# FFN up projection with the weights stationary and 256 tokens moving

## The chip, the core and the metric

The kernel runs on one core of a Trainium2 chip. Five engines of a core take part. TensorE does matmuls, VectorE, ScalarE and GpSimd work on elements, and SyncE issues most transfers. The metric is the device time of one run in microseconds (us). All arithmetic is on f32 data. A product of two f32 matrices is made of three TensorE passes in the type fp32r: each operand is split into a high part (a cast to fp32r) and a low part (the rest), and the passes are high x high, high x low and low x high.

## The reference, cut to what matters

Two layers, 256 tokens, model width 2048, feed-forward width 8192. What the change touches is the last line but one:

```python
def hybrid_layer(x, ...):
    ...
    mixed = jnp.concatenate([rms_norm(attn, g_attn_out), rms_norm(pool, g_pool_out)], axis=-1) @ w_out
    x = x + rms_norm(mixed, g_mix_post)
    f = jnp.square(jax.nn.relu(rms_norm(x, g_ffn_pre) @ w_up)) @ w_down
    return x + rms_norm(f, g_ffn_post)
```

`rms_norm(x, g)` is x times g over the root of the mean square of a token's row. The kernel applies g before the projection and the row's scale (`rstd`, one number a token) to its result.

## The kernel before, in words

**Tiles.** The 256 tokens are two halves (t = 0, 1) of 128. A weight matrix is taken in units of 512 output columns; a unit has 2048 rows of weights, in 8 slots of two blocks of 128 rows. Half 0 of a unit is slots 0 to 3, half 1 is slots 4 to 7. The feed-forward part of a layer is four groups (`group`, line 641). A group is four up units (512 features each) and then four down units that use these 2048 features.

**Weights.** SyncE loads 512 KB pieces into four buffers `raw` (line 303), each when VectorE has finished with the buffer. ScalarE casts a piece into `w_hi` (`split_hi`, line 687) once it has landed and TensorE has released the slot (`w_used`). VectorE subtracts it to make `w_lo` (`split_lo`, line 959), and TensorE waits for that (`lo_made`).

**A unit on TensorE** (`unit`, line 385, and `pair`, line 360). It goes first through all 8 slots for t = 0, then through all 8 for t = 1. A pair is one slot for one t and holds six passes. The stationary operand (128 x 128) is a block of tokens, and the moving operand is 512 columns of weights. The result is tokens on partitions and 512 features in one bank, `acc_bank[t]`. In the code, (n, p) counts the pairs: n = 0, 1 are the halves for t = 0, n = 2, 3 those for t = 1, and p is the slot of a half. The first pass of a bank waits for `acc_free[t]`, by which whoever reads the last result says that it is taken. A slot is released after its pair for t = 1, so all slots are needed in the first half of a unit and released in the second.

**After an up unit.** ScalarE reads the bank with relu and the row scale (line 902) and squares it (line 906). TensorE turns the 128 x 512 result in four transposes (`turn_f`, line 631) so that the features lie on partitions, as the down projection needs them for its stationary operand. ScalarE copies the turned bank as `f_hi` (line 911), VectorE makes `f_lo` (line 1221). The turn of t = 1 stands at (1, 2) of the following unit, the turn of t = 0 at (3, 2) of its own.

**After a down unit.** VectorE adds the bank into `acc` (`down_sum`, lines 1232 and 1234). The order that VectorE keeps in a down unit is written out:

```python
                    with dve.Fori(0, CHUNKS - 1 if last else CHUNKS) as c:
                        down_sum(g, c, 0, first)
                        split_lo(hu + 8 + c * 2 + 2, 0)
                        split_lo(hu + 8 + c * 2 + 3, 1)
                        down_sum(g, c, 1, first)
```

Each engine runs its instructions in the written order, and semaphores tie them together.

**The first up unit of a layer.** Its tokens for t = 1 are made ready while it runs (`h_first_unit`, line 410). The row scale of t = 1 comes late in it. ScalarE squares x (line 713) and does four casts, VectorE does four subtractions and then the mean (`mean_x`, line 1001; line 979), and GpSimd takes the root (line 1316). Before the change only ScalarE waits for this scale, in `activate` for t = 1.

## Time and profile before

| what | value |
|---|---|
| median of 3 runs | 2082.39 us (2081.54 to 2083.51) |
| span of the profiled execution | 2081.2 us |
| TensorE matmul busy | 2046.5 us, 98% |
| TensorE weight load busy | 1695.0 us, 81% |
| VectorE busy | 1088.2 us, 52% |
| ScalarE busy | 998.6 us, 48% |
| GpSimd busy | 212.1 us, 10% |

The page of the profile gives the span and no other time of that execution. Engines are named PE (TensorE matmul), PEld (TensorE weight load), DVE (VectorE), ACT (ScalarE), POOL (GpSimd) and SP (SyncE); L377 is line 377 of the kernel. Matmuls are pipelined, so the duration of one is longer than the distance to the next, and their ends are modelled. Starts are the better guide.

### The profile page before, as it was taken

The page shows a single profiled execution, that of the slowest core. Times are in us where ns is not written, and L with a number is a line of the kernel's source. Part 1 is how long each engine was busy: PE and PEld are TensorE (multiplying, and loading weights), DVE is VectorE, ACT ScalarE, POOL GpSimd, SP SyncE. Part 2 cuts the span into 40 slices and gives each one's busy share as a digit, 9 for nine tenths or more (in the row PEclk, how much of TensorE's full clock was granted, in tenths as well). Part 3 has the DMA queues.
Part 4 walks back from the last instruction along what each step waited for, and adds up shares of the span by engine and source line. Part 5 has one row for each costly group of instructions (what it writes and reads, how often), then busy time and mean ns, then how long its engine had stood idle before and what let it go on. Part 6 is the DMA issues. An engine that isn't in the chain of part 4 may idle for free.

```text
span 2081.2 us, 28816 instructions
## 1 busy us (share of the span) xinstructions
PE 2046.5 (98%) x9298; PEld 1695.0 (81%) x9298; DVE 1088.2 (52%) x1105; ACT 998.6 (48%) x1247; POOL 212.1 (10%) x248
## 2 busy tenths in 40 slices
PE   7999999999999999999989999999999999999998
PEld 5888887888888888888878888878888888888886
DVE  6554657554554554554554446664454454454454
ACT  5444656543553453454454446565345444444542
POOL 3951014000000000000120010230000000000001
PEclk9999999999999999999999999999999999999999
DMA  6664454565565555655556544555565566466463
GB/s 214 222 207 137 140 184 160 177 205 186 181 196 188 187 189 188 213 191 182 165 195 208 191 142 130 166 185 183 185 202 191 173 202 200 162 195 230 161 196 128
DMA packets 196518, 381.65 MB, mean 183 GB/s; under 512 B 11904, under 2 KB 14048, under 8 KB 195808
## 3 DMA queue, kind: packets, MB, share of 16 engines
q1 hardware_dynamic: 195776, 379.12, 55.7%
q10 hardware_dynamic: 672, 1.61, 0.2%
q8 instruction: 42, 0.69, 0.1%
q14 instruction: 28, 0.23, 0.0%
HBM read 378.59 MB, written 2.10 MB: 183 GB/s over the span
## 4 chain that ended last, share of the span: by engine, by line
PE 48%; issue 41%; POOL 8%; DMA 1%; DVE 0%; POOLq 0%; ACT 0%; SPq 0%; ACTq 0%; DVEq 0%
PE acc_bank L377 16%; PE acc_bank L379 16%; PE acc_bank L378 16%; POOL acc L1324 2%; POOL h_lo L1297 1%; PE t_bank L637 1%; POOL f_lo L1297 1%; DMA post_row<-in_g_ffn_post 1%; DMA x<-in_x 1%; POOL rstd L1316 0%; PE t_bank L405 0%; POOL band L1453 0%; POOL band L1447 0%; POOL tmp L1417 0%; POOL tmp L1423 0%
## 5 line engine op out<-in xcount | busy, mean ns | idle before, releaser
L964 DVE TENSOR_TENSOR w_lo<-raw,w_hi 128x1024 fp32r<-128x1024 f32 x704 | 871.5, 1250 | 573.4 <-ACT w_hi L692 538.9
L692 ACT CAST w_hi<-raw 128x1024 fp32r<-128x1024 f32 x704 | 734.1, 1052 | 481.7 <-PE acc_bank L379 265.9
L377 PE MATMUL acc_bank<-w_hi,h_hi 128*128 128x512 f32 x1536 | 608.9, 396 | 3.9 <-POOL h_lo L1297 2.2
L379 PE MATMUL acc_bank<-w_hi,h_lo 128*128 128x512 f32 x1536 | 600.0, 391 | 0.0
L378 PE MATMUL acc_bank<-w_lo,h_hi 128*128 128x512 f32 x1536 | 599.3, 390 | 0.0
L377 PE MATMUL acc_bank<-w_hi,f_hi 128*128 128x512 f32 x1216 | 477.4, 393 | 0.0
L379 PE MATMUL acc_bank<-w_hi,f_lo 128*128 128x512 f32 x1216 | 473.5, 389 | 0.0
L378 PE MATMUL acc_bank<-w_lo,f_hi 128*128 128x512 f32 x1216 | 473.1, 389 | 0.0
L377 PEld LDWEIGHTS acc_bank<-w_hi,h_hi 128*128 128x128 f32 x1536 | 289.8, 189 | 65.4 <-DVE w_lo L964 4.0
L379 PEld LDWEIGHTS acc_bank<-w_hi,h_lo 128*128 128x128 f32 x1536 | 289.0, 188 | 61.3
L378 PEld LDWEIGHTS acc_bank<-w_lo,h_hi 128*128 128x128 f32 x1536 | 289.7, 189 | 57.9
L379 PEld LDWEIGHTS acc_bank<-w_hi,f_lo 128*128 128x128 f32 x1216 | 228.2, 188 | 47.9
L378 PEld LDWEIGHTS acc_bank<-w_lo,f_hi 128*128 128x128 f32 x1216 | 228.4, 188 | 46.6
L377 PEld LDWEIGHTS acc_bank<-w_hi,f_hi 128*128 128x128 f32 x1216 | 228.3, 188 | 46.3
L1324 POOL TENSOR_TENSOR acc<-acc,post_row 128x512 f32<-128x512 f32 x32 | 43.2, 1353 | 1369.0 <-ACT junk L872 1369.0
L911 ACT CAST f_hi<-t_bank 128x512 f32 x64 | 37.6, 587 | 216.7 <-PE t_bank L637 216.7
L1221 DVE TENSOR_TENSOR f_lo<-t_bank,f_hi 128x512 f32 (+1 forms) x64 | 44.3, 692 | 186.0 <-ACT f_hi L911 186.0
L902 ACT ACTIVATE act_f<-acc_bank,rstd 128x512 f32<-128x512 f32 x64 | 43.8, 685 | 99.0 <-PE acc_bank L379 99.0
L1234 DVE TENSOR_TENSOR acc<-acc_bank,acc 128x512 f32 (+1 forms) x48 | 33.0, 688 | 99.2 <-PE acc_bank L379 99.2
L872 ACT ACTIVATE junk<-acc 128x512 f32<-128x512 f32 (+1 forms) x32 | 20.2, 632 | 93.0 <-DVE acc L1234 58.2
L1297 POOL TENSOR_TENSOR h_lo<-xg,h_hi 128x512 fp32r<-128x512 f32 x32 | 55.3, 1749 | 38.6 <-ACT h_hi L697 38.6
L1297 POOL TENSOR_TENSOR f_lo<-xg,f_hi 128x512 fp32r<-128x512 f32 x16 | 20.5, 1293 | 339.8 <-ACT f_hi L697 339.8
(150 smaller groups left out, 822.2 us busy)
## 6 DMA issues: line engine op xcount, KB each, us to landing
raw<-in_w_up SPq DMA_DIRECT2D x256, 512.0 KB, 4.4
raw<-in_w_down SPq DMA_DIRECT2D x256, 512.0 KB, 5.4
raw<-in_w_in SPq DMA_DIRECT2D x128, 512.0 KB, 4.8
raw<-in_w_out SPq DMA_DIRECT2D x64, 512.0 KB, 5.3
w_pool_s<-in_w_pool SPq DMA_DIRECT2D x2, 1024.0 KB, 8.5
post_row<-in_g_mix_post SPq DMA_DIRECT2D x2, 1024.0 KB, 7.3
post_row<-in_g_ffn_post SPq DMA_DIRECT2D x2, 1024.0 KB, 7.9
out<-x SPq DMA_DIRECT2D x8, 256.0 KB, 2.7
```

What stands on the lines that cost most here:

```text
L377: pe.matmul(bank[:, :], xh, wh, start=begin and k == 0, stop=False)
L378: pe.matmul(bank[:, :], xh, wl, start=False, stop=False)
L379: mm = pe.matmul(bank[:, :], xl, wh, start=False, stop=end and k == 1)
L637: tr = pe.transpose(t_bank[t][:, h_cols(j)], act_f[:, t, h_cols(j)], ident[:, :])
L692: act.copy(w_hi[:, half * PAIRS + p, :], raw[:, p, :]).then_inc(hi_made, 1)
L902: act.activation(act_f[:, t, :], acc_bank[t][:, :], ACT.Relu, scale=rstd[:, COL_X2 + t:COL_X2 + t + 1]).then_inc(acc_free[t], 1)
L911: act.copy(f_out(f_hi, u, t), t_bank[t][:, :].rearrange("p (k n) -> p k n", k=4)).then_inc(fhi_made, 1)
L964: dve.tensor_tensor(w_lo[:, slot, :], raw[:, p, :], w_hi[:, slot, :].bitcast(F32), ALU.subtract).then_inc(lo_made, 1)
L1221: dve.tensor_tensor(f_out(f_lo, u, t), t_bank[t][:, :].rearrange("p (k n) -> p k n", k=4), f_out(f_hi, u, t).bitcast(F32), ALU.subtract).t ...
L1234: dve.tensor_tensor(dst, acc_bank[t][:, :], dst, ALU.add).then_inc(acc_free[t], 1)
L1297: pool.tensor_tensor(lo, xg[:, slot, :].rearrange("p (k n) -> p k n", k=k), hi.bitcast(F32), ALU.subtract).then_inc(st_lo, 1)
L1324: pool.tensor_tensor(part, part, post_row[:, c_cols(c)], ALU.mult).then_inc(post_ready, 1)
```

## The change

All up units but the first of a layer change their order. A block of 128 x 128 weights is now the stationary operand and all 256 tokens are the moving one. One unit is 8 slots; a slot is four blocks of 128 features (n), two blocks of rows (k) and three passes of 256 columns, 24 passes in all. The result has features on partitions: blocks n = 0, 1 lie in the first bank of a pair of banks, n = 2, 3 in the second. Units take `acc_bank` and `s_bank` by turns (`up_bank`), so these units need no transposes. A slot is released as soon as its 24 passes are issued.

With tokens along the free axis the row scale is no longer one number a partition. In the first unit TensorE spreads it over the partitions (`spread_rstd`, before pair (3, 1)), and VectorE copies it to `rstd_row`. VectorE then takes an up result with relu and the row scale in one operation (`take_up`). ScalarE squares and casts it, VectorE subtracts (`up_lo`). The loop over the units of a group is written out in the program instead of a loop of the engine, on TensorE, ScalarE and VectorE. The first down unit takes `acc_bank`, while the last up unit lies in `s_bank`; hence its `spare`. In the cut below, empty lines are left out.

```diff
@@ -82,7 +82,7 @@
 TB_F = 18
-TB_LAYER = TB_F + FF_GROUPS * CHUNKS
+TB_LAYER = TB_F + 1
 XG_Y = 8
@@ -185,6 +185,7 @@
     act_f = at("act_f", [P, T, CH], F32, r_qkv)
+    rstd_row = at("rstd_row", [P, SEQ], F32, r_qkv + 4 * (T + 1) * CH + 4 * T * CH)
     post_row = own("post_row", [P, D])
@@ -272,9 +275,16 @@
     ld = bass.ds
-    def f_out(dst, u, t):
-        return dst[:, ld(u * 4, 4), h_cols(t)]
+    def f_turned(dst, t):
+        return dst[:, 0:4, h_cols(t)]
+    def f_part(dst, u, b):
+        return dst[:, 4 * u + 2 * b:4 * u + 2 * b + 2, :]
+    def up_bank(u, b):
+        return (acc_bank, s_bank)[u % 2][b]
     def result_stands(eng, t, result, hu):
...
-            def unit(hu, result, hi, lo, before=None):
+            def unit(hu, result, hi, lo, before=None, spare=0):
...
-                    pe.wait_ge(acc_free[t], result + 1)
+                    pe.wait_ge(acc_free[t], result + 1 - spare)
@@ -628,41 +638,75 @@
                                     h_turns(l, 1, (2, 3))
-                def turn_f(g, u, t):
-                    pe.wait_ge(f_ready, l * 32 + g * 8 + u * 2 + t + 1)
-                    pe.wait_ge(flo_made, l * 32 + g * 8 + u * 2 + t + 1)
+                def turn_first(t):
+                    pe.wait_ge(f_ready, l * T + t + 1)
                     for j in range(4):
                         tr = pe.transpose(t_bank[t][:, h_cols(j)], act_f[:, t, h_cols(j)],
                                           ident[:, :])
                     tr.then_inc(tb_done[t], 1)
+                def spread_rstd():
+                    pe.wait_ge(rstd_ready, T + l * RS_LAYER + RS_X2 + T)
+                    for t in range(T):
+                        mm = pe.matmul(o_bank[:, h_cols(t)],
+                                       rstd[:, COL_X2 + t:COL_X2 + t + 1].to_broadcast([P, P]),
+                                       ident[:, :], start=True, stop=True)
+                    mm.then_inc(row_done, 1)
+                def up_unit(hu, u, result, before=None):
+                    for s in range(2 * PAIRS):
+                        half, p = s // PAIRS, s % PAIRS
+                        if before is not None:
+                            before(s)
+                        pe.wait_ge(lo_made, (hu + half) * PAIRS + p + 1 + RAW)
+                        for n in range(4):
+                            b = n // 2
+                            dst = up_bank(u, b)[:, (n % 2) * SEQ:(n % 2 + 1) * SEQ]
+                            if s == 0 and n % 2 == 0:
+                                pe.wait_ge(acc_free[b], result + (1 if u == 0 else 0))
+                            for k in range(2):
+                                kt = 2 * s + k
+                                col = k * CH + n * P
+                                wh = w_hi[:, s, col:col + P]
+                                wl = w_lo[:, s, col:col + P]
+                                begin = s == 0 and k == 0 and n % 2 == 0
+                                end = s == 2 * PAIRS - 1 and k == 1 and n % 2 == 1
+                                pe.matmul(dst, wh, h_hi[:, kt, :], start=begin, stop=False)
+                                pe.matmul(dst, wh, h_lo[:, kt, :], start=False, stop=False)
+                                mm = pe.matmul(dst, wl, h_hi[:, kt, :], start=False, stop=end)
+                            if s == 2 * PAIRS - 1 and n == 1:
+                                mm.then_inc(acc_done, 1)
+                        mm.then_inc(w_used, 1)
                 def group(g, first, last):
                     hu = hu0 + HU_F + g * HU_GROUP
                     r = a0 + ACC_F + g * (2 * CHUNKS)
-                    h_before = h_first_unit(l, 1) if first else None
-                    def up_first(n, p):
-                        if h_before is not None:
+                    if first:
+                        h_before = h_first_unit(l, 1)
+                        def up_first(n, p):
                             h_before(n, p)
-                        if (n, p) == (3, 2):
-                            turn_f(g, 0, 0)
-                    unit(hu, r, h_hi, h_lo, up_first)
-                    with pe.Fori(1, CHUNKS) as u:
-                        def up_next(n, p):
-                            if (n, p) == (1, 2):
-                                turn_f(g, u - 1, 1)
+                            if (n, p) == (3, 1):
+                                spread_rstd()
                             if (n, p) == (3, 2):
-                                turn_f(g, u, 0)
-                        unit(hu + u * 2, r + u, h_hi, h_lo, up_next)
+                                turn_first(0)
+                        unit(hu, r, h_hi, h_lo, up_first)
+                    for u in range(1 if first else 0, CHUNKS):
+                        def up_next(s):
+                            if first and u == 1 and s == 1:
+                                turn_first(1)
+                        up_unit(hu + u * 2, u, r + u, up_next)
                     def down_first(n, p):
-                        if (n, p) == (1, 2):
-                            turn_f(g, CHUNKS - 1, 1)
-                        if p == 0:
-                            pe.wait_ge(flo_made, T + l * 32 + g * 8 + (3, 7, 4, 8)[n])
+                        if n < 2:
+                            pe.wait_ge(flo_made, l * 32 + g * 8 + max(2, 4 * n + p + 1))
                     def down_last(n, p):
@@ -670,7 +714,8 @@
                                 h_turns(l + 1, 0, (0, 1) if n == 2 else (2, 3))
-                    unit(hu + 2 * CHUNKS, r + CHUNKS, f_hi, f_lo, down_first)
+                    unit(hu + 2 * CHUNKS, r + CHUNKS, f_hi, f_lo, down_first, 1)
                     with pe.Fori(1, CHUNKS - 1 if last else CHUNKS) as c:
@@ -894,37 +939,51 @@
                 mix_square(1, 3)
-                def activate(g, u, t):
+                def activate_first(t):
                     act.wait_ge(rstd_ready, T + l * RS_LAYER + RS_X2 + t + 1)
-                    result_stands(act, t, a0 + ACC_F + g * 8 + u,
-                                  hu0 + HU_F + g * HU_GROUP + u * 2 + 1)
+                    result_stands(act, t, a0 + ACC_F, hu0 + HU_F + 1)
                     act.activation(act_f[:, t, :], acc_bank[t][:, :], ACT.Relu,
                                    scale=rstd[:, COL_X2 + t:COL_X2 + t + 1]
                                    ).then_inc(acc_free[t], 1)
-                    act.wait_ge(acc_free[t], 1 + a0 + ACC_F + g * 8 + u + 1)
+                    act.wait_ge(acc_free[t], 1 + a0 + ACC_F + 1)
                     act.activation(act_f[:, t, :], act_f[:, t, :], ACT.Square
                                    ).then_inc(f_ready, 1)
-                def f_chunk_hi(g, u, t):
-                    act.wait_ge(tb_done[t], l * TB_LAYER + TB_F + g * 4 + u + 1)
-                    act.copy(f_out(f_hi, u, t), t_bank[t][:, :].rearrange("p (k n) -> p k n", k=4)
+                def turned_hi(t):
+                    act.wait_ge(tb_done[t], l * TB_LAYER + TB_F + 1)
+                    act.copy(f_turned(f_hi, t), t_bank[t][:, :].rearrange("p (k n) -> p k n", k=4)
                              ).then_inc(fhi_made, 1)
+                def up_first(hu):
+                    activate_first(0)
+                    split_hi(hu + 2, 0)
+                    turned_hi(0)
+                    split_hi(hu + 3, 1, (0, 1, 2))
+                    activate_first(1)
+                    split_hi(hu + 3, 1, (3,))
+                    turned_hi(1)
                 def up_unit(g, u, hu):
-                    activate(g, u, 0)
                     split_hi(hu + 2, 0)
-                    f_chunk_hi(g, u, 0)
-                    split_hi(hu + 3, 1, (0, 1, 2))
-                    activate(g, u, 1)
-                    split_hi(hu + 3, 1, (3,))
-                    f_chunk_hi(g, u, 1)
+                    split_hi(hu + 3, 1)
+                    i = l * 2 * (FF_GROUPS * CHUNKS - 1) + 2 * (g * CHUNKS + u - 1)
+                    for b in range(2):
+                        act.wait_ge(acc_free[b], 1 + a0 + ACC_F + g * 8 + u + 1)
+                        act.activation(act_f[:, b, :], act_f[:, b, :], ACT.Square
+                                       ).then_inc(squared, 1)
+                        act.wait_ge(squared, i + b + 1)
+                        act.copy(f_part(f_hi, u, b),
+                                 act_f[:, b, :].rearrange("p (k n) -> p k n", k=2)
+                                 ).then_inc(fhi_made, 1)
                 def group(g, first, last):
                     hu = hu0 + HU_F + g * HU_GROUP
                     if first:
                         h_first_unit(l, 1, hu)
-                    with act.Fori(0, CHUNKS) as u:
+                        up_first(hu)
+                    for u in range(1 if first else 0, CHUNKS):
                         up_unit(g, u, hu + u * 2)
@@ -1014,7 +1073,6 @@
             dve.sem_inc(lo_made, RAW)
-            dve.sem_inc(flo_made, T)
             dve.memset(ones[:, :], 1.0).then_inc(ones_made, 1)
@@ -1215,13 +1273,36 @@
                 split_lo(hu_f + 1, 1, (1,))
-                def f_chunk_lo(g, u, t):
-                    dve.wait_ge(fhi_made, l * 32 + g * 8 + u * 2 + t + 1)
-                    dve.tensor_tensor(f_out(f_lo, u, t),
+                def turned_lo(t):
+                    dve.wait_ge(fhi_made, l * 32 + t + 1)
+                    dve.tensor_tensor(f_turned(f_lo, t),
                                       t_bank[t][:, :].rearrange("p (k n) -> p k n", k=4),
-                                      f_out(f_hi, u, t).bitcast(F32), ALU.subtract
+                                      f_turned(f_hi, t).bitcast(F32), ALU.subtract
                                       ).then_inc(flo_made, 1)
+                def take_row():
+                    dve.wait_ge(row_done, l + 1)
+                    dve.tensor_copy(rstd_row[:, :], o_bank[:, 0:SEQ]).then_inc(row_ready, 1)
+                def take_up(g, u):
+                    for b in range(2):
+                        result_stands(dve, b, a0 + ACC_F + g * 8 + u,
+                                      hu0 + HU_F + g * HU_GROUP + u * 2 + 1)
+                        dve.scalar_tensor_tensor(
+                            act_f[:, b, :].rearrange("p (k n) -> p k n", k=2),
+                            up_bank(u, b)[:, :].rearrange("p (k n) -> p k n", k=2), 0.0,
+                            rstd_row[:, None, :].to_broadcast([P, 2, SEQ]), ALU.max, ALU.mult
+                            ).then_inc(acc_free[b], 1)
+                def up_lo(g, u):
+                    for b in range(2):
+                        dve.wait_ge(fhi_made, l * 32 + g * 8 + u * 2 + b + 1)
+                        dve.tensor_tensor(f_part(f_lo, u, b),
+                                          act_f[:, b, :].rearrange("p (k n) -> p k n", k=2),
+                                          f_part(f_hi, u, b).bitcast(F32), ALU.subtract
+                                          ).then_inc(flo_made, 1)
                 def down_sum(g, c, t, first):
@@ -1237,19 +1318,21 @@
                     hu = hu0 + HU_F + g * HU_GROUP
-                    def up_unit(u, at_start):
-                        split_lo(hu + u * 2 + 2, 0)
-                        if at_start:
-                            mean_x(l, 1, 1)
-                        f_chunk_lo(g, u, 0)
-                        split_lo(hu + u * 2 + 3, 1)
-                        f_chunk_lo(g, u, 1)
                     if first:
                         h_first_unit(l, 1, hu)
-                        up_unit(0, True)
-                    with dve.Fori(1 if first else 0, CHUNKS) as u:
-                        up_unit(u, False)
+                        split_lo(hu + 2, 0)
+                        mean_x(l, 1, 1)
+                        turned_lo(0)
+                        take_row()
+                        split_lo(hu + 3, 1)
+                        turned_lo(1)
+                        dve.wait_ge(row_ready, l + 1)
+                    for u in range(1 if first else 0, CHUNKS):
+                        split_lo(hu + u * 2 + 2, 0)
+                        split_lo(hu + u * 2 + 3, 1, (0, 1, 2))
+                        take_up(g, u)
+                        split_lo(hu + u * 2 + 3, 1, (3,))
+                        up_lo(g, u)
                     with dve.Fori(0, CHUNKS - 1 if last else CHUNKS) as c:
```

## Rows read from the trace of the kernel before

**Rows 1.** The page, part 1: busy time, share of the span, instructions.
```profile
PE 2046.5 (98%) x9298; PEld 1695.0 (81%) x9298; DVE 1088.2 (52%) x1105; ACT 998.6 (48%) x1247; POOL 212.1 (10%) x248
```
**Rows 2.** Groups: line, engine, names, count, busy us, mean ns, idle before.
```profile
L377 PE MATMUL acc_bank<-w_hi,h_hi 128*128 128x512 f32 x1536 | 608.9, 396 | 3.9 <-POOL h_lo L1297 2.2 <-issue 0.8 <-DVE w_lo L964 0.7
...
L637 PE MATMUL t_bank<-ident,act_f 128*128 128x128 f32 x256 | 38.3, 271 | 0.0
```
**Rows 3.** Timeline (start us, us, engine, line), TensorE in a down unit.
```profile
800.02 0.39 PE L378 MATMUL acc_bank<-w_lo,f_hi 128*128 128x512 f32 x1
...
802.74 0.39 PE L378 MATMUL acc_bank<-w_lo,f_hi 128*128 128x512 f32 x1
```
**Rows 4.** Windows: busy us (count) by engine, clock, DMA; up phase, group 1.
```profile
507.10:597.50 90.40, 90.40 (x413) 74.80 (x413) 43.73 (x40) 44.81 (x53) 0.00 (x0) 1.00 0.56 184
```
**Rows 5.** Timeline, TensorE around the first turn of an up unit.
```profile
347.83 0.40 PE L379 MATMUL acc_bank<-w_hi,h_lo 128*128 128x512 f32 x1
348.06 0.60 PE L637 MATMUL t_bank<-ident,act_f 128*128 128x128 f32 x4
...
348.74 0.39 PE L378 MATMUL acc_bank<-w_lo,h_hi 128*128 128x512 f32 x1
```
**Rows 6.** Timeline, weight loads of eight short plain f32 operations, three places.
```profile
231.41 1.02 PEld L528 LDWEIGHTS t_bank<-ident,probs 128*128 128x128 f32 x8
232.40 0.19 PEld L377 LDWEIGHTS acc_bank<-w_hi,f_hi 128*128 128x128 f32 x1
...
239.03 1.71 PEld L517 LDWEIGHTS s_bank<-qk_t 128*128 128x128 f32 x8
240.76 0.19 PEld L377 LDWEIGHTS acc_bank<-w_hi,f_hi 128*128 128x128 f32 x1
...
277.24 1.08 PEld L620 LDWEIGHTS ssa_bank<-ones,o_sqsum 128*128 128x128 f32 x8
278.24 0.19 PEld L377 LDWEIGHTS acc_bank<-w_hi,f_hi 128*128 128x128 f32 x1
```
**Rows 7.** Timeline at the start of an up group, first and last of six.
```profile
507.14 0.39 PE L377 MATMUL acc_bank<-w_hi,h_hi 128*128 128x512 f32 x1
...
508.94 1.05 ACT L692 CAST w_hi<-raw 128x1024 fp32r<-128x1024 f32 x1 [0.23 <-DMA raw<-in_w_up]
...
507.46 3.79 DVE L964 TENSOR_TENSOR w_lo<-raw,w_hi 128x1024 fp32r<-128x1024 f32 x3 [1.10 <-ACT w_hi L692]
511.17 0.68 DVE L1232 COPY acc<-acc_bank 128x512 f32 x1
...
1893.76 0.39 PE L377 MATMUL acc_bank<-w_hi,h_hi 128*128 128x512 f32 x1
...
1898.45 0.68 DVE L1234 TENSOR_TENSOR acc<-acc_bank,acc 128x512 f32 x1
```
**Rows 8.** Timeline of the first up unit; last row: the same in layer 1.
```profile
346.47 0.39 PE L379 MATMUL acc_bank<-w_hi,h_lo 128*128 128x512 f32 x1
...
352.66 0.15 DVE L979 TENSOR_SCALAR_CACHE_REDUCE ss_x<-ss_x 128x4 f32<-128x4 f32 x1
...
352.90 0.55 POOL L1316 TENSOR_TENSOR rstd<-mean_sq,minus_half 128x1 f32<-128x1 f32 x1 [7.86 <-DVE ss_x L979]
...
1383.66 0.55 POOL L1316 TENSOR_TENSOR rstd<-mean_sq,minus_half 128x1 f32<-128x1 f32 x1 [7.86 <-DVE ss_x L979]
```
**Rows 9.** Timeline and windows (clock third from the end) after two idle times.
```profile
32.12 0.50 PE L377 MATMUL acc_bank<-w_hi,h_hi 128*128 128x512 f32 x1 [2.16 <-POOL h_lo L1297]
...
332.43 1.97 PE L405 MATMUL t_bank<-ident,x 128*128 128x128 f32 x8 [2.40 <-DVE x L991]
...
332.00:335.50 3.50, 3.07 (x12) 2.78 (x13) 3.50 (x7) 1.47 (x5) 0.04 (x1) 0.53 0.41 139
...
32.40:35.50 3.10, 3.10 (x19) 2.60 (x19) 1.35 (x3) 0.41 (x1) 1.36 (x1) 1.00 0.02 5
```
**Rows 10.** The page, part 3: a queue of instructions, packets, MB, share.
```profile
q8 instruction: 42, 0.69, 0.1%
```

6 lines of the change are left out of this document (4 added, 2 removed).

## The prediction

> **What bounds the kernel now.** I read the busy shares first: TensorE works for 98% of the span [rows 1], so time can come or go only through what TensorE issues and what it waits for. The grouped lines come next. They say how many passes there are of each kind, and that hardly any idle time stands before them [rows 2]. They do not give the cost of a pass, since its recorded duration (396 ns) overlaps the next one. The pace is read from start times instead: twelve passes of 512 columns from 800.02 to 802.74, or 226.7 ns each [rows 3]. An up phase of four units lasts 90.40 us [rows 4]. Its 4 x 96 passes are 87.05 us of that, and its seven blocks of four turns are the other 3.35 us, 0.48 us a block. The timeline agrees: 347.83 to 348.74 is 0.91 us for two passes and a block, so 0.46 us for the block, and the passes behind it are a little slow [rows 5]. So the up phase is TensorE alone, with nothing in it that waits.
>
> **Passes.** 30 units (15 of each layer) go from 96 passes of 512 columns to 192 of 256. The columns stay the same, but there are twice as many weight loads and twice as many pass starts. Before: 2880 x 0.2267 = 652.9 us. After: 5760 times a pace that the trace does not show for these operands, so I bound it.
> The load alone is one bound. Eight loads with one moving column each take 277.24 to 278.24. The first one begins with the pass before it (0.227), so the other seven cost 0.110 us each [rows 6]. No pace below about 110 ns has a row with this kind of operand.
> The stream is the other bound. Plain f32 turns with 128 columns take (0.99 - 0.227)/7 = 0.109 each, and plain f32 passes with 256 columns take (1.73 - 0.227)/7 = 0.215 [rows 6]. That is a line of 0.83 ns a column and 2.5 ns a pass, with the load hidden behind the stream in both. If the passes of this kernel have the same 2.5 ns fixed, their columns cost (226.7 - 2.5)/512 = 0.438 ns, and 256 columns cost 114.6 ns. If instead the whole surcharge over the ideal stream (226.7 - 213.3 = 13.4 ns, with 2.4 GHz being the granted clock of 1.00 in the window [rows 4]) falls on each pass or on each load, 256 columns cost 106.7 + 13.4 = 120.0 ns.
> I take 114.6, because it is built on the only two sizes of one kind that the trace has: 660.1 us, **+7.2 us**. The ends are 110 ns (633.6 us, -19.3) and 120 ns (691.2 us, +38.3).
> The Trainium skill (TensorE: Matmul & The Clock Gate, Back-to-back issue gap) gives a warm gap of columns/2.4 + 2.5 ns. For 256 columns that is an estimate of 109.2 ns, or 629.0 us. For 512 columns the rule says 215.8 ns, and this trace has 226.7 [rows 3], so it does not hold for these operands at the size that can be checked. It is rival C.
>
> **Turns.** 60 of 64 blocks go (two of each unit but the first of a layer): 60 x 0.48 = **-28.8 us** (-27.6 by the timeline's 0.46). ScalarE's copies from the turned bank and VectorE's subtractions give way to work of like number. Both engines are about half busy in an up phase (44 and 45 of 90 us [rows 4]), so this costs nothing as long as TensorE does not come to wait for them.
>
> **The wait at the start of groups 1 to 3.** The old order needed the second bank only halfway through a unit, 10.9 us in. The new one needs both banks within the first weight slot: the start of n = 2 waits for `acc_free[1]` after 12 short passes, 1.4 us in. For u = 0 the bank still holds the second half of the last down result. Its taker, `down_sum(.., 1)`, is queued on VectorE behind four subtractions that wait for ScalarE's casts, and the last cast waits for the last pass of the down unit. Nothing of this queue is changed. At the first such place the up unit begins at 507.14, the last cast runs from 508.94, and VectorE takes the bank at 511.17 to 511.85, while TensorE needs it at 507.14 + 1.38 = 508.52: 3.3 us of idle. At the last one it begins at 1893.76 and the bank is free at 1899.13: 4.0 us [rows 7]. The six places (three a layer) are 3.3, 3.3, 3.5, 3.5, 3.3 and 4.0 by the same subtraction: **+21.0 us**. Today 10.9 us of passes on the first bank cover this; with that cover gone all of it is on the path. For u > 0 the banks alternate, and TensorE waits only for a result two units old, which is hidden. The first down unit needs the last up result at n = 1, p = 2, which is 8.2 us in; square, copy and subtraction of two halves behind the last weight split are some 5 us by the durations of rows 7 and the 0.6 to 0.7 us of a 512-wide operation. Also hidden.
>
> **The wait in the first unit.** `spread_rstd` stands on TensorE before the pair (3, 1) and waits for both row scales. Until now only ScalarE waited for the second one. The pair before it issues its last pass at 346.47, so TensorE comes there at 346.70. VectorE makes the mean square at 352.66 and GpSimd the root at 352.90 to 353.45 [rows 8]: 6.8 us of idle. What makes it late is upstream and unchanged (ScalarE's eight squares, then four casts and four subtractions ahead of the mean). In layer 1 the root ends at 1384.21 [rows 8], 6.8 us after the same point. **+13.6 us.** Queued behind the waiting instruction on TensorE are the last three pairs of the unit and the turn, and ScalarE's copy from the turn waits for them. That shifts both engines' splits by the same 7 us, while the next unit wants its slots 4 to 7 only 10.9 us after its start, so I add nothing for it. The spread itself is four f32 instructions a layer near 0.11 us: **+0.9 us**.
>
> **The clock.** After 2.40 us idle at 332.43 the granted clock is 0.53 over the next 3.5 us: the lower level, 1.2 GHz. After 2.16 us idle at 32.12 it stays at 1.00 [rows 9]. About 3 us at half rate lose 1.5 us. All eight new waits are longer than 2.40 us, so I count 8 x 1.5 = **+12.0 us**; the ends are 0 and 12.
>
> **Sum.** 7.2 - 28.8 + 21.0 + 13.6 + 0.9 + 12.0 = +25.9 us on the span of 2081.2 is 2107.1. The page gives no other time of the profiled execution; the median of the runs is 1.2 us above its span, and I carry that over: **2108.3 us**, 1.2% slower.
>
> **Rivals.**
> A, the forecast: 45%, 2108.3.
> B, the surcharge belongs to the pass or to the load, 120 ns: 38.3 in place of 7.2, 2139.4. For it: each load now lies beside the whole stream instead of half of it. Against: plain f32 passes show only 2.5 ns fixed, also with a load to each. 30%.
> C, the other side: a short pass pays no surcharge and goes at 109.2 ns. Then the passes give 23.9 us back, the sum is -5.2, and the time 2077.2. It decides from 110.1 ns down, where 652.9 - 18.7 us (the other terms) over 5760 passes balances. Against: the load alone costs 110 and the long passes pay 11 ns more than this. 9%.
> D, the bank wait does not appear, because the subtractions ahead of `down_sum` run earlier than now: -21.0 and six clock drops of 1.5 less, 2078.3. For it: the last cast waits partly for its data, which could come sooner. Against: that cast can't begin before the down unit's last pass. 7%.
> E, the change does the passes but TensorE is not fed. The loops over units are written out, so program text that was fetched once and run three times is now fetched each time. The page has 42 transfers of 16 KB for instructions, 0.1% of 16 engines' span [rows 10], which is some 33 us or 0.8 us each. At most about as many more, none hidden, are +31: 2139. In this trace none shows as idle time of TensorE. 5%.
> F: The Trainium skill (TensorE: Matmul & The Clock Gate, "What overlaps and what doesn't") says a load overlaps a running pass only if the row groups differ; here they are all the full array. As a mechanism of this kernel, load and stream in series are 110 + 109 = 219 ns a short pass, +609 us, 2692. The rows are against it: 512 columns and a load would be over 320 ns, and the pace is 226.7 [rows 3]. 1%. Some 3% is left to slower cases not named.
>
> **Numbers.** The likeliest is A. Its low neighbours (no clock drops 2096; pace 110 as well, 2070) and D set the low end at 2080, B and part of E the high end at 2145. What a measurement of this kernel can tell from no change is 0.2%, 4.2 us. C, at 2077.2, is just beyond it and D, at 2078.3, just within it. Faster 9%, same 8%, slower 83%.
>
> **What would show it.** Start-to-start time of 256-column passes inside an up unit: 114 to 115 (A), 120 (B), 109 (C). Idle time of TensorE before the third output block of each group's first up unit, ended by VectorE's down sum, 3.3 to 4.0 us, six times. About 6.8 us twice before the spread, ended by GpSimd's root. Granted clock near 0.5 right after each. Turn blocks: four left. I am wrong if the short passes go at 110 or below, or if TensorE's idle time does not rise by some 35 us.

## The result and the profile after

The changed kernel takes 2142.02 us (median of 4 runs, 2138.23 to 2144.73) against 2081.97 before: a ratio of 1.0287, 95% interval 1.0275 to 1.0300. It is slower by 60 us where 26 were forecast. The profiled span goes from 2081.2 to 2136.5, +55.3. The profiled execution is the fastest of the four (2138.23). Two others took 6 us longer, with a mean granted clock of 0.985 instead of 0.991, so some 5 of the 60 us do not show in the trace.

The page of the changed kernel, part 1 (busy us, share, count) and its row for instruction fetches, against [rows 1] and [rows 10]:
```profile
PE 2067.4 (97%) x11946; PEld 1830.0 (86%) x11946; DVE 1126.8 (53%) x1167; ACT 960.5 (45%) x1187; POOL 208.5 (10%) x248
...
q8 instruction: 86, 1.41, 0.3%
```
TensorE's share of busy time fell by only one point, and its busy time rose by 21 us. So both suspects are there: dearer passes and new idle time. The groups by line tell them apart, as in [rows 2]:
```profile
L680 PE MATMUL s_bank<-h_hi,w_hi 128*128 128x256 f32 x1024 | 289.9, 283 | 0.0
...
L680 PE MATMUL acc_bank<-h_hi,w_hi 128*128 128x256 f32 x896 | 257.3, 287 | 21.3 <-DVE acc L1315 10.7 <-DVE acc L1313 7.3 <-DVE w_lo L1023 3.3
...
L645 PE MATMUL t_bank<-ident,act_f 128*128 128x128 f32 x16 | 3.3, 346 | 0.0
L653 PE MATMUL o_bank<-ident,rstd 128*128 128x128 f32 x8 | 2.4, 461 | 13.3 <-POOL rstd L1399 13.3
```
The turns fell from 256 to 16 instructions. The two new waits are here with their releasers: 18.0 us before passes on `acc_bank` that VectorE's down sums end (10.7 + 7.3; none on `s_bank`, since a group starts with `acc_bank`), and 13.3 us before the spread. The 3.3 us that the same row puts down to `w_lo` are something else, a branch, and come up below. The mean of 287 ns beside 283 says that some `acc_bank` passes ran slowly.

The pace inside an up unit (start us, us), to be set against [rows 3]:
```profile
539.95 0.28 PE L680 MATMUL acc_bank<-h_hi,w_hi 128*128 128x256 f32 x1
...
541.15 0.28 PE L681 MATMUL acc_bank<-h_lo,w_hi 128*128 128x256 f32 x1
```
Ten passes in 1.20 us: 120 ns each, as are 5590 of the 5750 spacings between two such passes in the trace.

The timeline at the first group start and at the first spread, the places of [rows 7] and [rows 8]:
```profile
521.84 0.68 DVE L1313 COPY acc<-acc_bank 128x512 f32 x1
...
522.58 0.58 PE L680 MATMUL acc_bank<-h_hi,w_hi 128*128 128x256 f32 x1 [3.54 <-DVE acc L1313]
...
352.59 0.54 POOL L1399 TENSOR_TENSOR rstd<-mean_sq,minus_half 128x1 f32<-128x1 f32 x1 [7.85 <-DVE ss_x L1038]
353.19 1.22 PE L653 MATMUL o_bank<-ident,rstd 128*128 128x128 f32 x4 [6.65 <-POOL rstd L1399]
```
What the clock did after them, in windows (length, busy and count of PE, PEld, DVE, ACT, POOL, then granted clock, DMA share, GB/s), as in [rows 9]:
```profile
353.20:357.00 3.80, 3.80 (x12) 3.11 (x13) 0.00 (x0) 0.00 (x0) 0.00 (x0) 0.50 0.93 330
522.60:526.00 3.40, 3.40 (x16) 3.40 (x17) 0.00 (x0) 0.46 (x1) 0.00 (x0) 0.52 0.81 299
...
707.45:711.00 3.55, 3.55 (x30) 3.55 (x31) 0.81 (x1) 1.05 (x1) 0.00 (x0) 1.00 0.81 284
```
16 passes in 3.4 us is little more than half the rate of 30 in 3.55. The clock was at its lower level, 1.2 GHz, after the waits of 6.7 and 3.5 us. After the wait at 707.4, which is 2.0 us, it stayed at 2.4 GHz. After the spread's wait the low stretch is longer than after a bank wait. The next window has 0.80 over 4 us, which is 1.6 us more at the lower level, so TensorE ran slowly for 5.4 us:
```profile
357.00:361.00 4.00, 4.00 (x18) 3.39 (x17) 2.52 (x4) 3.14 (x4) 0.00 (x0) 0.80 0.01 4
```

The middle groups run in a loop that is now longer than before. At the loop's closing branch stands a new piece of idle time. TensorE's own queue at that line (shortest, median and longest in ns; first and last start), and windows of the down phase that ends there and of the up phase behind it:
```profile
L725 PEldq COMPARE_BRANCH  x4: 67/2582/5102, 698.2 to 1939.6; - x4
```
```profile
614.85:703.73 88.88, 87.23 (x387) 71.90 (x385) 44.75 (x42) 35.56 (x36) 0.00 (x0) 1.00 0.54 179
```
```profile
703.73:798.21 94.48, 92.49 (x769) 92.29 (x770) 49.26 (x47) 40.60 (x45) 0.00 (x0) 1.00 0.62 189
```
The branch that is taken lasts 5.1 us (once a layer). It begins at 698.2. Sixteen more passes start behind that, the last at 701.67, so they cover 3.7 us. The branch ends at 703.3 and the next pass starts at 703.70: 1.8 us are idle, 88.88 against 87.07 of the other down phases. A 16 KB transfer of the instruction queue q8 begins at 700.9, inside the branch. The kernel before has none there. The profile names `w_lo` as what ended this idle time (3.3 us in two places, in the row above), because a subtraction ended at 703.60. By VectorE's order that one is for a later slot, and the first pass does not wait for it.

The ledger by phases. An up phase of group 1 or 3 lasts 97.4 (before 90.41), one of group 2 94.4, a first up phase 107.2 (before 96.55), a down phase 87.07 (before 87.54, as it too lost a turn block), and the two with the branch 88.88. Together these phases are 57.3 us longer. As terms: passes +38.3, turns -28.8, bank waits +19.0, spread waits +13.6, spread +0.9, branch +3.6, which sum to 46.6. That leaves 10.7 us for the clock. By rows, the six low stretches come to 11.4: about 1.5 us for each of the four after bank waits, and half of 5.4, 2.7 us, for each of the two after the spread. The stages that the change does not touch were 2.0 us shorter in this execution: 57.3 - 2.0 = 55.3.

The small rest fits with the kernel before: two low stretches that it had in its first up units are gone, though nothing was changed at their place. Before, the granted clock fell after 2.40 us of idle at 332.43 [rows 9]. In the changed kernel TensorE was idle for 2.41 us up to 332.55, and the clock stayed at 1.00.

### The profile page after: what moved, and what is told of

Its sections match the earlier page's. It is cut to its first block, busy times and chain, and to the rows that moved or that the text cites. A ratio compares the mean times of both kernels' runs of the same rounds, so it can differ in the third digit from the quotient of the medians.

```text
span 2136.5 us, 33613 instructions
## 1 busy us (share of the span) xinstructions
PE 2067.4 (97%) x11946; PEld 1830.0 (86%) x11946; DVE 1126.8 (53%) x1167; ACT 960.5 (45%) x1187; POOL 208.5 (10%) x248
## 4 chain that ended last, share of the span: by engine, by line
PE 45%; issue 43%; POOL 8%; DMA 2%; DVE 1%; ACT 1%; POOLq 0%; DVEq 0%; SPq 0%; ACTq 0%
PE acc_bank L387 7%; PE acc_bank L389 7%; PE acc_bank L388 7%; PE s_bank L682 4%; PE s_bank L680 4%; PE s_bank L681 4%; PE acc_bank L680 4%; PE acc_bank L681 4%; PE acc_bank L682 4%; POOL acc L1407 2%; POOL h_lo L1380 1%; DMA raw<-in_w_up 1%; POOL f_lo L1380 1%; DMA post_row<-in_g_ffn_post 1%; DMA x<-in_x 1%
## 5 line engine op out<-in xcount | busy, mean ns | idle before, releaser
L680 PE MATMUL s_bank<-h_hi,w_hi 128*128 128x256 f32 x1024 | 289.9, 283 | 0.0
L682 PE MATMUL s_bank<-h_hi,w_lo 128*128 128x256 f32 x1024 | 289.8, 283 | 0.0
L681 PE MATMUL s_bank<-h_lo,w_hi 128*128 128x256 f32 x1024 | 289.8, 283 | 0.0
L680 PE MATMUL acc_bank<-h_hi,w_hi 128*128 128x256 f32 x896 | 257.3, 287 | 21.3 <-DVE acc L1315 10.7
L681 PE MATMUL acc_bank<-h_lo,w_hi 128*128 128x256 f32 x896 | 256.2, 286 | 0.0
L682 PE MATMUL acc_bank<-h_hi,w_lo 128*128 128x256 f32 x896 | 256.0, 286 | 0.0
L387 PE MATMUL acc_bank<-w_hi,h_hi 128*128 128x512 f32 x576 | 231.2, 401 | 5.8 <-POOL h_lo L1380 4.0
L388 PE MATMUL acc_bank<-w_lo,h_hi 128*128 128x512 f32 x576 | 226.7, 394 | 0.0
L389 PE MATMUL acc_bank<-w_hi,h_lo 128*128 128x512 f32 x576 | 226.6, 393 | 0.0
L680 PEld LDWEIGHTS s_bank<-h_hi,w_hi 128*128 128x128 f32 x1024 | 196.6, 192 | 0.1
```

Source lines behind the costliest of these rows:

```text
L387: pe.matmul(bank[:, :], xh, wh, start=begin and k == 0, stop=False)
L388: pe.matmul(bank[:, :], xh, wl, start=False, stop=False)
L389: mm = pe.matmul(bank[:, :], xl, wh, start=False, stop=end and k == 1)
L680: pe.matmul(dst, wh, h_hi[:, kt, :], start=begin, stop=False)
L681: pe.matmul(dst, wh, h_lo[:, kt, :], start=False, stop=False)
L682: mm = pe.matmul(dst, wl, h_hi[:, kt, :], start=False, stop=end)
```

## The experiments

All ratios are against the kernel before, run on the same chip.

**e_narrow: the pace alone.** The kernel before, with each pass of 512 columns of the 30 up units issued as two of 256 (cut):
```diff
-pe.matmul(bank[:, :], xh, wh, ...)
+for a, b in ((0, SEQ), (SEQ, 2 * SEQ)):
+    pe.matmul(bank[:, a:b], xh, wh[:, a:b], ...)
```


> The kernel before with one thing changed: in the 30 up units that the change touches, each pass of 512 moving columns is two of 256, tokens still stationary, turns and all waits as before. Theory P (each pass pays about 13.4 ns over its ideal stream, whatever its width): 256 columns go at 120 ns here too, 5760 x 0.120 - 2880 x 0.2267 = +38 us, 2120 us. Rival W (the 120 ns come from the weights being the stationary operand, or from the token operand as the moving one): here the pace stays near 113 to 115 ns, 0 to +7 us, 2082 to 2089 us.


Measured 2117.59 (2116.49 to 2118.79), ratio 1.0174 [1.0158, 1.0191], +35.6 us. Its timeline, and the window of its first full up phase (before: [rows 4]):
```profile
739.92 0.28 PE L379 MATMUL acc_bank<-w_hi,h_hi 128*128 128x256 f32 x1
...
741.00 0.28 PE L379 MATMUL acc_bank<-w_hi,h_hi 128*128 128x256 f32 x1
```
```profile
509.72:604.88 95.16, 95.16 (x798) 95.12 (x797) 44.13 (x41) 45.48 (x54) 0.00 (x0) 1.00 0.53 178
```
Nine passes in 1.08 us: 120 ns, with the old roles of the operands and no wait in the phase (busy 95.16 of 95.16). The surcharge comes with the pass, whichever operand moves. This alone is more than half of the loss.

**e_bank: the last down sum ahead of one subtraction.**
```diff
-split_lo(hu + 8 + c * 2 + 3, 1)
-down_sum(g, c, 1, first)
+split_lo(hu + 8 + c * 2 + 3, 1, (0, 1, 2))
+down_sum(g, c, 1, first)
+split_lo(hu + 8 + c * 2 + 3, 1, (3,))
```


> The changed kernel with one thing moved: in every down unit VectorE takes the second bank before it subtracts the last weight slot, not after. Theory (TensorE waits at the start of groups 1 to 3 for this bank only): the waits of 3.6 us (four times) and 2.1 us (twice) go, about 18.5 us, and the 4 clock drops behind them, 6 us: about 24 us off, 2115 to 2119 us. Rival (the wait is for the last weight slot or for data, and the bank is only what came last): the idle time stays or moves to the weights, under 5 us off.


Measured 2131.48 (2130.25 to 2135.27), 1.0237 [1.0220, 1.0254]: 10.5 us off, where 24 were expected. What TensorE waited for (us, times, longest):
```profile
PE acc_bank L680 <- issue: 5.7, 2, 3.0
PE acc_bank L680 <- DVE acc L1315: 5.2, 2, 3.0
PE acc_bank L680 <- DVE acc L1313: 5.2, 2, 2.9
```
The waits for VectorE's sum fell from 18.0 to 10.4 us, in four places of six; those of group 2 are gone. The 5.7 us with `issue` are the idle time at the loop's branch, which grew from 3.3: the branch took 6.4 and 6.2 us in this execution, and 5.1 in the changed kernel's. At the first group start the subtractions still ahead of the sum are late, since their casts waited 1.5 and 0.8 us for weights to land. The place was right, but the edit was too small. It is repeated below, further forward.

**e_spread: the spread one unit later.** `spread_rstd()` moves from the pair (3, 1) of the first unit to slot 3 of unit 1, and VectorE takes the row there.


> The changed kernel with the spread of the row scales moved on TensorE from before pair (3, 1) of the first unit to the fourth slot of the second, and VectorE's copy of it behind its subtractions there. Theory: 6.8 us of idle and about 2.5 us of clock go in each layer, 17 to 19 us off, 2121 to 2126 us. Rival (the first unit is late for something else that would stop TensorE next, such as the weights behind ScalarE): half of that or less.


Measured 2138.30 (2134.63 to 2140.11), 1.0268 [1.0251, 1.0285], not the 2121 to 2126 of the theory. The spread's wait is gone, but a wait of 5.1 us stands at the next turn. Its timeline:
```profile
358.75 1.04 ACT L737 CAST w_hi<-raw 128x1024 fp32r<-128x1024 f32 x1 [1.13 <-DMA raw<-in_w_up]
...
360.32 1.04 ACT L737 CAST w_hi<-raw 128x1024 fp32r<-128x1024 f32 x1 [0.53 <-DMA raw<-in_w_up]
361.28 0.68 ACT L946 ACTIVATE act_f<-acc_bank,rstd 128x512 f32<-128x512 f32 x1
361.99 0.63 ACT L950 ACTIVATE act_f<-act_f 128x512 f32<-128x512 f32 x1
...
362.68 1.12 PE L645 MATMUL t_bank<-ident,act_f 128*128 128x128 f32 x4 [5.09 <-ACT act_f L950]
```
TensorE comes to the second turn 2.9 us into unit 1; before the change it was 8.2 us in. The prediction had not seen this, because the longer wait ahead of it hid it. The root is no longer what is late: GpSimd has it at 356.7. ScalarE comes to its activation only at 361.28, behind three casts that waited for weights to land.

**e_filled: the bank wait kept, but TensorE kept busy in it.** 26 passes of 256 columns into a bank that nobody reads, right before the wait:
```diff
+if s == 0 and n == 2 and u == 0:
+    for _ in range(26):
+        pe.matmul(ssa_bank[:, 0:SEQ], w_hi[:, 0, 0:P], h_hi[:, 0, :], start=True, stop=True)
```


> The changed kernel with 26 passes of 256 columns whose result nobody reads, put on TensorE before the wait for the second bank in groups 1 to 3 (3.1 us of work in a wait of 3.6; in the middle groups the wait is 2.1, so 1 us more there). Theory (part of the loss is the clock at 1.2 GHz after an idle wait): the work costs nothing where the wait is 3.6 us and the clock stays at 1.00 behind it: 4 x 1.5 - 2 x 1.0 = 4 us off, about 2136 to 2139 us, and the runs lie closer together. Rival (the clock drops for another reason, or the loss behind the wait is a refill): 2 us or more above the changed kernel, 2144 us.


Measured 2138.35 (2136.72 to 2142.15), 1.0278 [1.0261, 1.0296]. The interval overlaps that of the change, so the phases have to carry the reading. Timeline and window at the first place, to be set against 0.52 above:
```profile
518.89 3.28 PE L672 MATMUL ssa_bank<-h_hi,w_hi 128*128 128x256 f32 x26
522.61 0.39 PE L684 MATMUL acc_bank<-h_hi,w_hi 128*128 128x256 f32 x1 [0.44 <-DVE acc L1317]
```
```profile
522.50:526.00 3.50, 3.39 (x28) 3.39 (x29) 0.64 (x2) 1.05 (x1) 0.00 (x0) 1.00 0.90 327
```
The bank comes free at the same time, but the clock stays at 1.00. The up phases of groups 1 and 3 fall from 97.3 or 97.5 to between 95.7 and 96.3: 1.0 to 1.9 us each. This is the price of one clock drop behind a bank wait, for which the forecast took 1.5. Group 2, which had no drop, lost 1.0 and 2.4 us. The second of these holds a drop of its own, after 3.0 us of idle at the loop's branch.

**m_sizes: the pace of one size after another.** The kernel before with blocks of 48 passes behind its end, each pass with a stationary tile of its own; nobody reads their results. The cut shows one block, with W for its columns.
```diff
+for i in range(24):
+    pe.matmul(t_bank[i % 2][:, 0:W], h_hi[:, i % 16, 0:128], w_hi[:, i % 8, 0:W], ...)
+    pe.matmul(t_bank[i % 2][:, 0:W], h_lo[:, i % 16, 0:128], w_lo[:, i % 8, 0:W], ...)
```


> The kernel before with eleven blocks of 48 passes added at the end of TensorE's program, whose results nobody reads. High and low parts alternate, each pass has its own load. Moving columns 512, 384, 256, 128, 64 with a full stationary operand; 256 and 512 with only 64 and 32 stationary columns; the pair of a 512-column pass that moves the high and low tokens together and a 256-column pass; 256 columns with the same stationary operand each time. Theory P (13.4 ns a pass, fixed): 226.7, 173.4, 120.0, and then the load bound near 110 for 128 and 64; narrow stationary operands change nothing: 120 and 226.7. Theory L (the surcharge is the load's): with 64 or 32 stationary columns 256 goes at about 114 or 111 and 512 at about 220 or 218. Theory C (my prediction, 2.5 ns a pass and 0.438 a column): 170.7 for 384 and 114.6 for 256. The pair: 346.7 ns by P.


One run, 2160.96. Second and last of the 24 passes of one line, at W of 512, 384, 256 and 128:
```profile
2071.70 0.39 PE L685 MATMUL t_bank<-w_hi,h_both 128*128 128x512 f32 x1
2081.67 0.39 PE L685 MATMUL t_bank<-w_hi,h_both 128*128 128x512 f32 x1
2082.47 0.34 PE L688 MATMUL t_bank<-w_hi,h_both 128*128 128x384 f32 x1
2090.12 0.33 PE L688 MATMUL t_bank<-w_hi,h_both 128*128 128x384 f32 x1
2090.70 0.28 PE L691 MATMUL t_bank<-w_hi,h_both 128*128 128x256 f32 x1
2095.98 0.28 PE L691 MATMUL t_bank<-w_hi,h_both 128*128 128x256 f32 x1
2096.39 0.27 PE L694 MATMUL t_bank<-w_hi,h_both 128*128 128x128 f32 x1
2101.30 0.28 PE L694 MATMUL t_bank<-w_hi,h_both 128*128 128x128 f32 x1
```
Each pair of rows spans 44 passes: 226.6, 173.9, 120.0 and 111.6 ns. The first three are columns/2.4 plus 13.3, 13.9 and 13.3 ns: a fixed surcharge over 256 to 512 columns. The column model of the forecast (0.438 ns a column and 2.5) gives 170.7 and 114.6 for 384 and 256, and is refuted at both. At 128 columns the sum would be 66.7; there the load is the floor, near the 110 ns of [rows 6]. With 32 stationary columns in place of 128, 256 columns went at 113.3 ns, near what theory L has there, but 512 columns did not gain (231.7, where L has 218). With the same stationary tile named each time, 256 columns stayed at 119.8. A pair of a merged pass and a short one took 346.7 ns, as P has it. So the surcharge is the same from 256 to 512 columns with a full stationary tile, and what it is stays open. Some blocks are no measure of the pace: the granted clock was 0.50 from 2103.2 to 2113.5, in the blocks of 64 moving and of 64 stationary columns. It fell in the block of 64 moving columns, with TensorE busy all the time.

**e_unroll: the middle groups without their loop.** `with pe.Fori(1, FF_GROUPS - 1) as g` becomes a plain `for` on TensorE, ScalarE and VectorE.


> The changed kernel with groups 1 and 2 written out on TensorE, ScalarE and VectorE instead of a loop over the two. Theory (the branch back to the start of the middle group waits 5.1 us for its instructions to be fetched, of which 1.8 us show on TensorE in each layer): 3.6 us of idle go, but the bank wait of these two places, now 2.1 us, grows back to about 3.6 us, with its clock drop: 1 to 3 us back. Net -3 to +2 us, 2138 to 2143 us; the idle time ended by nothing in the profile before group 2 is gone. Rival (fetches hurt all along in written-out code): more instructions straight through cost time, over 2145 us.


Measured 2146.95 (2144.81 to 2147.51), 1.0310 [1.0294, 1.0325]: 4.9 us above the change and outside the stated 2138 to 2143. Its lowest run lies just above the highest of the change. The gap at the branch goes, as its window of the down phase shows:
```profile
614.72:701.79 87.07, 87.07 (x387) 72.12 (x386) 43.24 (x40) 34.66 (x35) 0.00 (x0) 1.00 0.52 177
```
But it had been a cover. With TensorE 1.8 us earlier, the bank wait of group 2 is back at full length and the clock drops behind it: its up phase goes from 94.4 to 97.3. Three of the four up phases of groups 1 and 3 rose too, to as much as 100.1, with waits up to 5.1 us at VectorE's sum. At the longest, ScalarE's last cast ahead of the sum waited 1.8 us for weights to land, where it waited 0.2 in the changed kernel. Why the weights came later is open. The time is where the rival had it (over 2145), but TensorE shows no idle time in its written-out code that only a fetch would explain.

**e_nostall: bank, spread and unroll together.**


> The changed kernel with the three repairs together: second bank taken early, spread moved to the second unit, groups 1 and 2 written out. Theory (the loss is 38 us of pace less 29 us of turns plus waits and clock): all waits gone, 2082 + 38.3 - 28.8 + 0.9 = 2092 us, still slower than before by 0.5%. Rival (there are further costs, such as fetches or weights that come late): 2097 us or more.


Measured 2124.35 (2121.85 to 2127.35), 1.0206 [1.0192, 1.0220]. 2092 was missed by 32 us, and the waits left, with clock drops behind some of them, say by what: 9.1 us at the second turn, 12.7 us at six bank waits of 2.1 on average.

**e_merged: two of the three passes merged.** On top of e_nostall, `h_hi` and `h_lo` lie side by side. One pass of 512 columns streams both against one load of `w_hi`, into the two halves of a bank; the pass with `w_lo` stays at 256. VectorE adds the halves.


> As the last one, but in the units with weights stationary the two passes that share the high part of the weights are one: it moves the high and the low tokens as 512 columns into the two halves of a bank, and VectorE adds the halves. Four banks a unit, two sets of four by turns. Theory P (13.4 ns a pass): two passes of 226.7 + 120.0 in place of three of 120, 1920 x 13.3 = 25.5 us off the last one: 2067 us, 0.7% faster than before. Rival C (cost by columns): nothing gained against the last one, 2092 us. Rival V (VectorE's extra work, some 3 us a unit, makes it late for the weights or the banks): waits of TensorE for VectorE come back, over 2075 us.


Measured 2101.36 (2098.30 to 2102.33), 1.0088 [1.0074, 1.0102], 34 us above the stated 2067. A third of the surcharges goes, and the up phases come to 91.59. A pair of passes takes 353 ns, not 226.7 + 120.0 = 346.7. The wait at the second turn is still there (9.2 us), and rival V came true in part: 5.9 us of waits for VectorE at the first down unit of groups 1 to 3, 1.0 each.

**e_turn: the order within unit 1.** On e_spread, the second turn moves from slot 1 to slot 3 of unit 1, and the spread to slot 5.
```diff
-if first and u == 1 and s == 1:
+if first and u == 1 and s == 3:
     turn_first(1)
-if first and u == 1 and s == 3:
+if first and u == 1 and s == 5:
     spread_rstd()
```


> The changed kernel with the second turn block of the first up group issued at the fourth chunk pair of unit 1 (8.6 us into the unit) and the spread of the root at its sixth. In the kernel that moved only the spread the wait of 6.7 us went and one of 5.1 us came at the turn block, which there comes 2.9 us into the unit. Theory 'the order within unit 1 is the whole matter': no wait of the first up group is left, each of its two phases falls by 6.7 of wait and by up to 1.5 of the slow clock from the changed kernel's 107.2 to about 99 to 100.5, and the kernel comes to 2125 to 2129. Rival 'VectorE and ScalarE are late as a whole in that unit, and whoever comes next waits': a wait of over 3 us appears at another instruction, phases of 103 or more, kernel at 2134 or more.


Measured 2127.39 (2122.70 to 2127.63), 1.0211 [1.0194, 1.0228], 14.6 us below the change. That is in the stated 2125 to 2129. No wait at the spread or at a turn is left in the first up group, whose phases fall from 107.2 to 97.8. The rival (whoever comes next waits) had been true of e_spread's place only. So nearly all of what the forecast had put down for the spread (13.6 us of waits and 3 of clock) was a matter of where eight instructions of a layer stand.

**e_nostall2: the new waits removed, short passes kept.** e_nostall with e_turn's places, and `down_sum(.., 1)` behind one subtraction of four.
```diff
-split_lo(hu + 8 + c * 2 + 3, 1, (0, 1, 2))
+split_lo(hu + 8 + c * 2 + 3, 1, (0,))
 down_sum(g, c, 1, first)
-split_lo(hu + 8 + c * 2 + 3, 1, (3,))
+split_lo(hu + 8 + c * 2 + 3, 1, (1, 2, 3))
```


> All waits attacked together, passes of 256 columns kept: the groups written out, spread and second turn as in the kernel above, and the second half's down sum on VectorE ahead of three splits rather than of one. Theory 'the change costs the fixed 13 ns a pass, and all else of it is waits that an order of instructions can remove': up phases of groups 1 to 3 at 90.42 + 5.12 - 3.37 = 92.2 plus what is left of the waits, below 93; first up group below 101; kernel at 2096 to 2101, which is the kernel before plus about 38 for pace less 29 for turns plus a few us. Rival 'the results of the last down unit are late by VectorE's own work, whatever the order': waits of 2 us stay at the group starts, phases of 94 to 96, kernel above 2108.


Measured 2092.88 (2092.22 to 2093.36), 1.0051 [1.0035, 1.0068]. The expectation named 92.2 for an up phase; the window of the first one:
```profile
510.13:602.28 92.15, 92.15 (x769) 92.11 (x768) 50.78 (x49) 41.33 (x46) 0.00 (x0) 1.00 0.63 198
```
All six are 92.15. The span is 2091.6, 10.4 above the 2081.2 of before, and passes, turns and spread alone are 38.3 - 28.8 + 0.9 = 10.4. The time itself fell 3 us below the stated 2096 to 2101. With this the ledger closes: 49 us of the 60 were waits, their clock drops and the branch, and all of them could go without touching the idea of the change. The up phases carry this (92.15 less 90.41 is the 1.74 that passes and turns give). That the span comes out at the very 10.4 is partly chance, since stages that no edit touches differ by 1 to 2 us between executions.

**e_merged2 and e_blocked: can it beat the kernel before?** e_merged with the same places as e_nostall2; then its passes in another order: in each slot first the eight of 512 columns, then the eight of 256.


> The kernel above with two of each three passes merged: one of 512 columns that streams the high and the low parts of 256 tokens against one weight load, then one of 256. The merged kernel measured 2101.4 with 9.2 us of waits at the second turn and 5.9 us at the group starts; with both gone, with the slow clock after the two turn waits (2 x 1.5), it comes to 2083 to 2087, at the kernel before (2082) or up to 0.25% above it. If its up phases stay at 91.6, what is left to the 90.4 of before is the pace of the pairs (353 ns for the two passes, of three at 240 in 720 before for twice the columns), and no wait.

> The kernel with the merged passes (2087.1, up phases 91.59 against 90.42 of the kernel before), with the passes of each two chunks in another order: first the eight of 512 columns, then the eight of 256, where it had them in turn; and the wait for the second half's banks at its own first pass. In turn, a pair of passes measured 353 ns (233 to 241 and 112 to 120), while the sum of the two paces measured alone is 226.7 + 120.0 = 346.7. Theory 'the extra 6.6 ns lie at the change from a short pass to a long one (a weight load that has only the short pass to hide in)': passes of 512 columns at 226.7, of 256 at 120, up phases at 256 x 0.3467 = 88.8 plus up to 1 of waits, seven or eight phases 1.8 to 2.8 shorter, and the kernel at 2067 to 2074, below the kernel before. Rival 'a pass of 512 columns that streams two stretches of SBUF, or starts a bank anew each time, costs 233 or more wherever it stands': the phases stay at 91 or more and the kernel at 2084 or more.


e_merged2 measured 2087.12 (2085.12 to 2090.61), 1.0026 [1.0015, 1.0036]: just above what was expected, with up phases of 91.59. The 5.9 us of waits that its expectation puts at the group starts stand at the first down units, and they stayed. e_blocked measured 2082.14 (2079.20 to 2083.46, 11 runs), 0.9997 [0.9988, 1.0006]: the same as the kernel before, not the 2067 to 2074 of its theory. Timeline and first up phase of e_blocked:
```profile
700.74 1.09 PE L677 MATMUL s_bank<-h_both,w_hi 128*128 128x512 f32 x4
701.67 0.62 PE L677 MATMUL o_bank<-h_both,w_hi 128*128 128x512 f32 x2
702.13 0.62 PE L677 MATMUL ssa_bank<-h_both,w_hi 128*128 128x512 f32 x2
702.58 0.64 PE L682 MATMUL s_bank<-h_both,w_lo 128*128 128x256 f32 x4
...
703.54 1.09 PE L677 MATMUL s_bank<-h_both,w_hi 128*128 128x512 f32 x4
```
```profile
509.18:599.82 90.64, 89.52 (x513) 78.62 (x513) 59.36 (x76) 43.39 (x47) 0.00 (x0) 1.00 0.65 202
```
Eight pairs in 2.80 us are 350 ns a pair. The 256-column passes go at 120 (703.54 - 702.58 over eight), the long ones at 230 (1.84 over eight). Both theories hold by half. Turn and turn about cost 3 ns a pair more than blocks of eight (353 against 350). Within a block, a long pass with another long one behind it takes 230.5 ns on average, and the last one, with a short one behind it, 226.7. So it is not slower wherever it stands, and in m_sizes a pair took 346.7. What makes the difference is open. Another 1.1 us a phase (89.52 busy of 90.64) waits at the first down unit for VectorE's extra additions.

## Why the prediction was right or wrong, point by point

- **The step that failed is "I take 114.6".** The passes cost 120.0 ns, +38.3 us in place of +7.2, 31 us too few. The span as a whole missed 29. The rest nearly cancels: bank waits 2 less than forecast, clock 1.3 less, the branch 3.6 more with no term of its own, and the unchanged stages 2.0 shorter by chance. Rival B had this number and its reason (13.4 ns on each pass). The choice rested on carrying the 2.5 ns of plain f32 operations [rows 6] over to operands of another kind. The two sizes of that line were of the wrong kind, and for the right kind the trace had one size, 512 [rows 3]. One size can't tell a slope from a fixed part, and the two ends deserved even odds at least. e_narrow and m_sizes both say that it is fixed.
- **Rival C and the rule behind it.** The Trainium skill (TensorE: Matmul & The Clock Gate, Back-to-back issue gap) gives columns/2.4 + 2.5 ns as the gap of an isolated pass, which is an estimate of 109.2 for 256 columns. This case measures 120.0, and 173.9 for 384 columns where it would say 162.5. It does not hold for these operands. Doubt was right; the surcharge was only put in the wrong place.
- **Turns, -28.8:** right. 16 instructions are left, and e_nostall2's phases agree to 0.1 us.
- **The bank waits, 21.0:** right in place and releaser, and in number to 2 us. Start to start, less a pace, those of groups 1 and 3 are 3.6 to 3.9 us and those of the middle group 2.0 and 2.1, together 19. The middle ones were shorter because TensorE came 1.8 us late itself. Rival D is out, yet its idea was sound as a cure: moved far enough, the down sum comes in time.
- **The spread's wait, 13.6:** right (7.03 us start to start less a pace of 0.23, twice; 13.3 in the profile's view), ended by GpSimd's root. What was missed is that the second turn was the next thing late, by 5.1 us, hidden behind it.
- **The clock, 12.0:** some 11, but partly by luck. There were six drops behind the new waits and not eight. The price of one behind a bank wait was right (e_filled, 1.0 to 1.9); behind the spread it was 2.7. The two middle waits of 2.0 and 1.9 us had none. The premise, taken from one row, that 2.40 us of idle brings the clock down is not safe: in other runs it fell after 1.96 us (e_turn) and 2.18 (e_nostall), and stayed up after 2.41 (the changed kernel) and 3.04 (e_bank). After every wait of 3.3 us or more it fell.
- **Rival E, fetches:** its mechanism came true in part. There were 86 transfers and not 42. All of the exposed time stood at one place that the rival had not named: the closing branch of the loop over groups, 1.8 us twice. In the variants that keep the loop, the branch took 4.8 to 6.5 us, with 1.5 to 3.2 exposed. The Trainium skill (Runtime: NRT & Kernel Launch, Instruction fetch mechanics) says that a taken branch to a target outside the instructions held forces a fetch before execution can go on; the branch of 5.1 us agrees, and its gap is gone in e_unroll. Written-out units by themselves showed no gap.
- **Rival F** is out: a pass of 120 ns holds load and stream together. (Its 2692 leaves out the other terms, +18.7 us; with them it would have been 2710.)
- **The sum.** The profiled span came to 2136.5, and the four runs reach 2144.7; the range of 2080 to 2145 held them at its very edge.

## What to carry to other kernels

Before trading few wide passes for many narrow ones, get the fixed cost of a pass from two sizes of the very operand kind; from one size, work with both ends. When a change makes TensorE need a bank or a result earlier, price the wait, but first ask whether moving the late producer or the early consumer by some instructions removes it, and look for the wait that stands next in line. A clock drop came on top of every wait of 3.3 us or more here, and on top of some between 2.0 and 3.2, so a shorter wait can save more than its own length.

## What the runs showed of the hardware that was not expected

- Passes of this kind at full clock: columns/2.4 ns + 13.4 ns from 256 to 512 columns (226.6, 173.9, 120.0), 111.6 at 128. Plain f32 passes of 256 columns take 215 ns, and 128 and 256 columns lie on a line with only 2.5 ns fixed [rows 6].
- After 3.5 us idle the granted clock was at its lower level for some 3 us, after 6.7 us for 5.4. After 2.4 us idle at one and the same place it fell in the kernel before and not in the changed one.
- The granted clock also fell with TensorE busy all the time, in passes of 64 moving columns (m_sizes, 2103.2).
- A loop's closing branch took 5.1 us when taken, with 3.7 us covered by the sixteen passes that still started behind its beginning.
- A merged pass of 512 columns over two stretches of SBUF took 230.5 ns on average with another one behind it, and 226.7 with a short pass behind it (e_blocked).
